# Block 1's one-hot rows: VectorE compares, GpSimd multiplies the columns' side by the weights

## The chip, the cores and the metric

The kernel is one program on one core of a Trainium2 chip. Its time is the device time of one execution in microseconds (us), the median of several executions. The core has five engines with their own instruction streams: TensorE (PE in the profile, its weight loads PEld), VectorE (DVE), ScalarE (ACT), GpSimd (POOL) and SyncE (SP). They work on SBUF, 128 partitions wide, and TensorE writes its results to PSUM. An engine takes its instructions in order, and semaphores tie the engines together. Sixteen DMA engines move data between HBM and SBUF; transfers are issued from the queues of SP and POOL here.

## The reference

One layer of a streaming encoder for 256 tokens of width 2048: a token-mixing part (an SSD branch and an attention branch, gated and merged), then a channel-mixing part. Only the second matters here, and of it only the end:

```python
def peer_ffn(h, w_q, keys_1, keys_2, u_table, v_table):
    ...
    top_score, top_pos = lax.top_k(cand_score, PEER_TOPK)
    expert = jnp.take_along_axis(cand_index, top_pos, axis=-1)   # index = i1 * 128 + i2
    gate = jax.nn.softmax(top_score, axis=-1)
    ...
        u = jnp.take(u_table, e_blk, axis=0)
        act = jax.nn.gelu(jnp.einsum('td,ted->te', h_blk, u), approximate=False)
        v = jnp.take(v_table, e_blk, axis=0)
        return jnp.einsum('te,ted->td', g_blk * act, v)
```

Each token chooses 8 x 16 = 128 of the 128 x 128 experts. Its output is the sum of 128 rows of the table v (16384 rows of 2048 numbers), each times a weight g * act. Everything is float32.

## The kernel before

The 256 tokens are two blocks of 128 (b = 0, 1), a token to a partition. The sum over v is made in two ways, one for each half of the width.

- **The right half (columns 1024 to 2047)** is gathered: for each of the 256 pairs of block and choice, r = 0 to 255, GpSimd issues an indirect DMA (`gather`, L2103, 512 KB) into one of the 8 slots of `vrow`, and VectorE adds the row times its weight to an accumulator in PSUM (`add_row`, L1965 and L1968). Row r can be gathered only once row r - 8 is added (semaphore `vrow_used`).
- **The left half (columns 0 to 1023)** is dense: every row of the table goes through TensorE (L990, 1024 products of 128x512, with units of 1 MB of the table in the 4 slots of `vden`, loaded from SP). The matrix that it is multiplied by, `wt`, holds each token's weight for each of the 16384 experts. It is made here in advance.

`wt` is made token by token. For a token the 128 choices lie on the partitions. Two one-hot matrices are formed, one row to each choice: o[0] has a 1 at column i1 (the rows' side), o[1] at column i2 (the columns' side), and o[1] is then multiplied by the choice's weight. One product of the two, 128x128, is the token's weight matrix. Four tokens (OHT = 4) are a group; a block has 32 groups (OHB = 32), n = 0 to 31. A group's one-hots fill one of two buffers, `oh[b][:, n % 2]`.

For block 0 ScalarE makes the one-hots, and the sum over v waits. For block 1 VectorE does, and its loop is what the change touches. Once block 0 and all rows of the table u are done (the scores' rows `rrow`, L1937), each group of block 1 goes like this:

- VectorE compares (L1981, 128x1024 for both sides of four tokens), waits for its own result (`link`), and multiplies the columns' side by the weights `selT[:, 2]` (L1983, 128x512). That sets `oh_ready`. From n = 2 on the comparison first waits for `wt_done` of group n - 2, since it writes into that group's buffer.
- TensorE takes four products (L981) and sets `wt_done`.
- ScalarE copies the result from PSUM into `wt1a` and `wt1b` (L1331) and sets `wt_read`.
- After every fourth group VectorE adds one gathered row (`add_row(n // 4)`, L1985). GpSimd has issued rows 0 to 7 before, and issues one more behind each added row.

After the last group VectorE runs through the rest of the 256 rows and TensorE through the dense half; the fourth slot of `vden` lies on the one-hots' buffers, so SP loads it only when all products of the one-hots are done. At the end VectorE forms the residual and the last LayerNorm (L1992 to L2014), and SP stores.

Of the kernel before, what the change touches and what calls it, by code (L numbers as in the profile page):

```python
# [12 lines left out]
ALU = mybir.AluOpType  # L13
# [4 lines left out]
P = 128  # L18
D = 2048
SEQ = 256  # L20
BLK = SEQ // P
# [82 lines left out]
class Steps:  # L104
# [14 lines left out]
    def link(self, ins):  # L119
        self.step(ins)  # L120
        self.wait()
# [9 lines left out]
def build(nc, a, out, stop="all"):  # L131
    ctx = ExitStack()
    with ctx:
        KB = 1024

        def at(name, offset, shape, dt=F32):
            return nc.alloc_sbuf_tensor_at(name, shape, dt, offset=SBUF_START + int(offset))
# [10 lines left out]
        def sem(name):  # L148
            return ctx.enter_context(nc.semaphore(name))
# [114 lines left out]
        ROWS = 8  # L264
# [24 lines left out]
        SEL = PEER_HEADS * TOPK  # L289
# [3 lines left out]
        niota = cos2[:, :, :].rearrange("p b n -> p (b n)")  # L293

        selT = at("selT", 206 * KB, [P, 3, P])

        OHT, OHB = 4, P // 4
        oh = [at("oh0", 102 * KB, [P, 2, 2, OHT, P]), at("oh1", 70 * KB, [P, 2, 2, OHT, P])]
# [9 lines left out]
        def wt_column(b, q):  # L308
            return wt[b][0][:, q, :] if b == 0 or q < QA else wt[b][1][:, q - QA, :]
# [37 lines left out]
        ada_in_ready = sem("ada_in_ready")  # L347
        rows_turned = sem("rows_turned")
        cols_ready = sem("cols_ready")
        c_hi_ready = sem("c_hi_ready")  # L350
        c_ready = sem("c_ready")
        x_normed = sem("x_normed")
        x_turned = sem("x_turned")
# [81 lines left out]
        square_done = sem("square_done")  # L435
        hot_done = sem("hot_done")
        oh_ready = sem("oh_ready")
        wt_done = sem("wt_done")
        wt_read = sem("wt_read")

# [21 lines left out]
        dve_step = sem("dve_step")  # L462
        act_step = sem("act_step")
        pool_step = sem("pool_step")
        probe_done = sem("probe_done")

# [9 lines left out]
        def on(phase):  # L478
            return order.index(phase) <= upto
# [120 lines left out]
        def _(pe):  # L600
# [143 lines left out]
            if on("att"):  # L744
                pe.wait_ge(cn_split, 2)
                pe.wait_ge(kpe_read, 1)
                with pe.Fori(0, 4) as i:
                    for k in range(2):
# [10 lines left out]
                        n = (U_ATT + k) % 2  # L759
                        rope = [w[:, n, :, 0:2 * QH].rearrange("p kc (e m) -> p kc e m", e=2)[:, :, :, NOPE:QH]  # L760
                                for w in (whi, wlo)]
                        for b in range(BLK):
                            o = ps[:, 0, 0, b * 256 + k * P:b * 256 + k * P + P]
# [6 lines left out]
                    for k in range(2):  # L770
# [4 lines left out]
                        n = (U_ATT + 2 + k) % 2  # L775
                        val = [w[:, n, :, :].rearrange("p kc (e m) -> p kc e m", e=2)[:, :, :, NOPE:KVH]
                               for w in (whi, wlo)]
                        for b in range(BLK):
                            o = aux[:, b, k * 256:k * 256 + 256]
# [20 lines left out]
                    for h in range(4):  # L800

                        for b in range(BLK):
                            nk = P * (b + 1)
                            o = aux[:, h, b * P:b * P + nk]
# [161 lines left out]
            if on("all"):  # L966
                pe.wait_ge(score_a, 4)
                pe.wait_ge(score_v, 4)
                for b in range(BLK):
                    pe.wait_ge(w_ready, PEER_HEADS * (b + 1))  # L970
                    for k in range(3):
                        src = w_all[:, b * SEL:(b + 1) * SEL] if k == 2 else sides[:, k, b * SEL:(b + 1) * SEL]
                        last = nc.tensor.transpose(aux[:, 2, k * P:k * P + P], src, ident)  # L973
                    last.then_inc(sel_turned, 1)
                    for n in range(OHB):
                        m = b * OHB + n
                        pe.wait_ge(oh_ready, m + 1)
                        if m >= 2:
                            pe.wait_ge(wt_read, m - 1)
                        for t in range(OHT):  # L980
                            last = mm(aux[:, n % 2, t * P:t * P + P], oh[b][:, n % 2, 0, t, :], oh[b][:, n % 2, 1, t, :],  # L981
                                      start=True, stop=True)
                        last.then_inc(wt_done, 1)
                pe.wait_ge(wt_read, BLK * OHB)
                for u in range(NVU):
                    pe.wait_ge(vden_full[u % 4], vden_before[u % 4] + 16 * (u // 4 + 1))
                    for q in range(2):
                        for b in range(BLK):
                            for n in range(DV // W):
                                last = mm(aux[:, 2 * b + n, :], wt_column(b, 2 * u + q),  # L990
                                          vden[:, u % 4, q, n * W:n * W + W],
                                          start=(u == 0 and q == 0), stop=(u == NVU - 1 and q == 1))
                    last.then_inc(vden_used, 1)
# [389 lines left out]
        def _(dve):  # L1383
            V = nc.vector
            S = Steps(dve, dve_step)
            link = S.link
# [277 lines left out]
            if on("mla"):  # L1664
# [6 lines left out]
                with dve.Fori(0, 2) as i:  # L1671
                    S.enter(i, 4 + 2 * (DC - 1))
                    for s in range(2):
# [5 lines left out]
                        for k in range(2):  # L1679
                            m = premix[:, ds(i * 8 + (4 * s + 2 * k), 2), :]  # L1680
# [98 lines left out]
            if on("so"):  # L1779

                dve.wait_ge(g0_ready, 4)
                with dve.Fori(0, 2) as i:
                    S.enter(i, 4)
                    for s in range(2):
# [3 lines left out]
                        for k in range(2):  # L1788
                            m = ds(i * 8 + (4 * s + 2 * k), 2)
# [138 lines left out]
            if on("all"):  # L1928
# [30 lines left out]
                def add_row(r):  # L1959

                    o = ps[:, r // SEL, :, :].rearrange("p a n -> p (a n)")
                    row, w = vrow[:, r % ROWS, :], w_all[:, r:r + 1]
                    dve.wait_ge(vrow_full[r % ROWS], vrow_before[r % ROWS] + 16 * (r // ROWS + 1))
                    if r % SEL == 0:
                        last = V.tensor_scalar(o, row, w, None, ALU.mult)  # L1965
                    else:
                        dve.wait_ge(vrow_used, r)
                        last = V.scalar_tensor_tensor(o, row, w, o, ALU.mult, ALU.add)  # L1968
                    last.then_inc(vrow_used, 1)
# [6 lines left out]
                for n in range(OHB):  # L1976
                    if n >= 2:
                        dve.wait_ge(wt_done, OHB + n - 1)
                    o = oh[1][:, n % 2]
                    t4 = slice(n * OHT, n * OHT + OHT)  # L1980
                    link(V.tensor_tensor(o, niota.unsqueeze(1).unsqueeze(1).broadcast_to([P, 2, OHT, P]),  # L1981
                                         selT[:, 0:2, t4].unsqueeze(3).broadcast_to([P, 2, OHT, P]), ALU.is_equal))
                    V.tensor_tensor(o[:, 1], o[:, 1], selT[:, 2, t4].unsqueeze(2).broadcast_to([P, OHT, P]), ALU.mult)\  # L1983
                        .then_inc(oh_ready, 1)
                    if n % 4 == 3:  # L1985
                        add_row(n // 4)
                for r in range(OHB // 4, BLK * SEL):
# [31 lines left out]
        def _(pool):  # L2019
            G = nc.gpsimd  # L2020
# [79 lines left out]
            if on("all"):  # L2100
                def gather(dst, table, r):
                    pool.sem_inc(held, 1)
                    return G.indirect_dma_start(  # L2103
                        out=dst, out_offset=None, in_=table,
                        in_offset=bass.IndirectOffsetOnAxis(ap=eid_all[:, r:r + 1], axis=0))

                for r in range(BLK * SEL):
                    if r % TOPK == 0:
                        pool.wait_ge(expert_ready, r // TOPK + 1)
                    if r in (0, 1):  # L2110

                        pool.wait_ge(lo_ready, U_END + 3 + r)
                    if r == 4:

                        pool.wait_ge(pe_used, U_END + 2)
                    pool.wait_ge(row_used, r + 1)
                    gather(rrow[:, r % ROWS, :], a["peer_u"][0], r).then_inc(row_full[r % ROWS], 16)
                for r in range(BLK * SEL):
                    if r < ROWS:

                        pool.wait_ge(row_used, ROWS + BLK * SEL - ROWS + r // 2 + 1)
                    else:
                        pool.wait_ge(vrow_used, r - ROWS + 1)
                    gather(vrow[:, r % ROWS, :], a["p_vg"], r).then_inc(vrow_full[r % ROWS], 16)

    return nc

# [45 lines left out]
```

## Time and profile before

| What | Value |
|---|---|
| Median of 3 executions | 2972.63 us (2970.52 to 2976.9) |
| The profiled execution's own time | 2973.76 us |
| Its span, first to last instruction | 2972.0 us |
| Mean granted clock of TensorE | 0.835 of full speed |
| Busy time of PE, DVE, ACT, POOL | 2027.2, 2231.5, 868.8, 911.0 us |

All times in the rows are counted from the span's start. The profiled execution's time is 1.76 us longer than its span. Its granted clock is a share of full speed: 1.0 is the level 2.4 GHz, 0.5 is 1.2 GHz.

### The profile page before, as it was taken

To read this page: it belongs to the slowest core of one execution; us is meant where nothing else is said; L and a number is where in the kernel's file an instruction comes from. 1 tells how busy PE (TensorE), PEld (TensorE's weight loads), DVE (VectorE), ACT (ScalarE), POOL (GpSimd) and SP (SyncE) were. 2 spreads that over 40 slices of the span, in tenths; PEclk is the share of its full clock that TensorE was granted. 3 is DMA by queue.
4 is the path that set the end of the run, shared out by engine and by line. 5 is a ranking of instruction groups with operands and counts; after the bars stand their busy time and mean duration, and the time that the engine had idled before them with its cause. 6 is when DMAs were issued, how large, how long until landed. Compare 5 with 4: busy or idle time off the path is not lost.

```text
span 2972.0 us, 33711 instructions
## 1 busy us (share of the span) xinstructions
PE 2027.2 (68%) x11910; PEld 1659.2 (56%) x11910; DVE 2231.5 (75%) x2576; ACT 868.8 (29%) x1225; POOL 911.0 (31%) x725
## 2 busy tenths in 40 slices
PE   4589998999999999998968000001111269999991
PEld 3589998888888889998768000001111154444440
DVE  7757677788878784445565999999999997666568
ACT  1144442344444444333342000004554620000000
POOL 0000001222222220001001656565656724444343
PEclk9799999999999999999989555555555569999995
DMA  8656668666555554655534888898989949999996
GB/s 340 281 181 203 209 212 307 218 219 208 207 200 205 200 194 170 228 182 213 183 139 188 322 356 342 336 364 330 367 326 366 378 159 367 413 414 414 415 413 235
DMA packets 144932, 817.42 MB, mean 275 GB/s; under 512 B 16520, under 2 KB 21248, under 8 KB 70832
## 3 DMA queue, kind: packets, MB, share of 16 engines
q0 software_dynamic: 93200, 477.21, 41.3%
q1 hardware_dynamic: 49728, 336.05, 30.5%
q10 hardware_dynamic: 1888, 2.59, 0.2%
q8 instruction: 76, 1.25, 0.2%
q14 instruction: 40, 0.33, 0.0%
HBM read 811.55 MB, written 4.23 MB: 274 GB/s over the span
## 4 chain that ended last, share of the span: by engine, by line
PE 38%; DVE 34%; DMA 14%; issue 8%; ACT 2%; POOL 1%; DVEq 1%; ACTq 0%; POOLq 0%
DVE rrow L1937 16%; DMA vrow<-in_p_vg,acc 12%; PE ps L639 9%; PE ps L641 9%; PE ps L640 9%; DVE ps L1968 3%; DVE wlo L1392 2%; DVE acc L1441 2%; ACT whi L1006 2%; PE ps L619 2%; PE ps L621 2%; PE ps L620 2%; DMA ada_in<-in_p_ada 1%; DVE oh L1981 1%; PE aux L898 1%
## 5 line engine op out<-in xcount | busy, mean ns | idle before, releaser
L1392 DVE TENSOR_TENSOR wlo<-raw,whi 128x2048 fp32r<-128x2048 f32 x216 | 507.5, 2352 | 375.6 <-ACT whi L1006 365.5
L2103 POOL DMA_INDIRECT rrow<-in_peer_u,acc x256 | 471.6, 1842 | 490.5 <-DVE dots L1937 205.8
L1006 ACT ACTIVATE whi<-raw 128x2048 fp32r<-128x2048 f32 x216 | 412.8, 1913 | 706.4 <-PE ps L641 483.7
L1937 DVE CUSTOM_DVE_ANT_0 rrow<-rrow,h 128x2048 f32<-128x2048 f32 x256 | 567.7, 2286 | 2.6 <-issue 1.7
L639 PE MATMUL ps<-h_hi,whi 128*128 128x256 f32 (+1 forms) x1568 | 454.5, 290 | 8.2 <-issue 4.2
L1968 DVE SCALAR_TENSOR_TENSOR ps<-vrow,acc,ps 128x1024 f32<-128x1024 f32 x254 | 327.2, 1288 | 162.3 <-DMA vrow<-in_p_vg,acc 144.6
L640 PE MATMUL ps<-h_lo,whi 128*128 128x256 f32 (+1 forms) x1568 | 444.7, 284 | 0.0
L641 PE MATMUL ps<-h_hi,wlo 128*128 128x256 f32 (+1 forms) x1568 | 444.7, 284 | 0.0
L2103 POOL DMA_INDIRECT vrow<-in_p_vg,acc x256 | 248.8, 972 | 315.1 <-DVE ps L1968 233.3
L981 PE MATMUL aux<-oh 128*128 128x128 f32 x512 | 116.0, 401 | 304.6 <-ACT oh L1350 281.8
L639 PEld LDWEIGHTS ps<-h_hi,whi 128*128 128x128 f32 (+1 forms) x1568 | 300.4, 192 | 21.2 <-issue 13.3
L640 PEld LDWEIGHTS ps<-h_lo,whi 128*128 128x128 f32 (+1 forms) x1568 | 300.4, 192 | 4.0 <-issue 3.8
L641 PEld LDWEIGHTS ps<-h_hi,wlo 128*128 128x128 f32 (+1 forms) x1568 | 300.2, 191 | 0.0
L2033 POOL DMA_DIRECT2D ada_in<-in_p_ada x128 | 69.3, 542 | 750.8 <-DVEq L1542 601.3
L973 PE MATMUL aux<-con,sides 128*128 128x128 f32 x4 | 1.4, 442 | 413.1 <-DVE acc L1949 413.1
L981 PEld LDWEIGHTS aux<-oh 128*128 128x128 f32 x512 | 100.7, 293 | 320.3 <-ACT oh L1350 291.4
L990 PE MATMUL aux<-vden,wt 128*128 128x512 f32 x512 | 242.5, 596 | 5.4 <-DMA vden<-in_p_vd 4.7
L973 PEld LDWEIGHTS aux<-con,sides 128*128 128x128 f32 x4 | 0.6, 204 | 413.5 <-issue 398.9
L1441 DVE SCALAR_TENSOR_TENSOR acc<-ada_in,csil,acc 128x512 f32<-128x512 f32 x240 | 203.4, 848 | 25.3 <-DMA ada_in<-in_p_ada 11.7
L990 PE MATMUL aux<-vden,wt1a 128*128 128x512 f32 x384 | 180.4, 592 | 0.0
L619 PE MATMUL ps<-whi,h_hi 128*128 128x512 f32 x320 | 133.6, 418 | 55.7 <-DVE wlo L1392 55.7
L990 PEld LDWEIGHTS aux<-vden,wt 128*128 128x128 f32 x512 | 97.6, 191 | 128.5 <-issue 122.1
(329 smaller groups left out, 4002.4 us busy)
## 6 DMA issues: line engine op xcount, KB each, us to landing
raw<-in_p_in SPq DMA_DIRECT2D x104, 1024.0 KB, 5.1
ada_in<-in_p_ada POOLq DMA_DIRECT2D x128, 512.0 KB
vden<-in_p_vd SPq DMA_DIRECT2D x64, 1024.0 KB, 8.6
ada_in<-in_p_ada SPq DMA_DIRECT2D x32, 1024.0 KB, 10.1
raw<-in_p_so SPq DMA_DIRECT2D x32, 1024.0 KB, 4.9
raw<-in_p_mo SPq DMA_DIRECT2D x16, 1024.0 KB, 6.8
raw<-in_p_bc SPq DMA_DIRECT2D x16, 1024.0 KB, 4.9
raw<-in_p_mix SPq DMA_DIRECT2D x16, 1024.0 KB, 4.9
```

The source lines that it names most:

```text
L619: mm(outs[b], x_hi[:, k, t], hi[:, kc, 0:width], start=(k == 0), stop=False)
L639: mm(o, wh, x_hi[:, k, :], start=(k == 0 and first), stop=False, skip_group_check=True)
L640: mm(o, wh, x_lo[:, k, :], start=False, stop=False, skip_group_check=True)
L641: last = mm(o, wl, x_hi[:, k, :], start=False, stop=(k == klast), skip_group_check=True)
L981: last = mm(aux[:, n % 2, t * P:t * P + P], oh[b][:, n % 2, 0, t, :], oh[b][:, n % 2, 1, t, :], start=True, stop=True)
L990: last = mm(aux[:, 2 * b + n, :], wt_column(b, 2 * u + q), vden[:, u % 4, q, n * W:n * W + W], start=(u == 0 and q == 0), stop=(u == NVU - ...
L1006: F(whi[:, n % 2, :, 0:cols_], raw[:, n % 4, :, 0:cols_], ACT.Copy).then_inc(hi_ready, 1)
L1392: V.tensor_tensor(wlo[:, n % 2, :, 0:cols_], raw[:, n % 4, :, 0:cols_], whi[:, n % 2, :, 0:cols_].bitcast(F32), ALU.subtract).then_inc(lo_ ...
L1441: last = V.scalar_tensor_tensor(acc_, tile[:, kc, :], csil[:, k:k + 1], acc_, ALU.mult, ALU.add)
L1937: last = V.tensor_tensor_reduce(row, row, h2[:, b, :], 1.0, 0.0, ALU.mult, ALU.add, dots[:, k, e:e + 1])
L1968: last = V.scalar_tensor_tensor(o, row, w, o, ALU.mult, ALU.add)
L2103: return G.indirect_dma_start(out=dst, out_offset=None, in_=table, in_offset=bass.IndirectOffsetOnAxis(ap=eid_all[:, r:r + 1], axis=0))
```

## The change

The loop on VectorE keeps the comparison alone and signals it by a new semaphore, `oh_equal`. GpSimd takes the multiplication, waits for `oh_equal`, and signals `oh_weighted`, for which TensorE now waits in block 1. GpSimd's gathers of rows 8 to 14 now stand in between, in places written out by hand: behind the multiplications of groups 5, 9, ..., 29. `oh_ready` belongs to block 0 alone, where n + 1 is the count that was m + 1.

```diff
@@ TensorE
                     for n in range(OHB):
                         m = b * OHB + n
-                        pe.wait_ge(oh_ready, m + 1)
+                        pe.wait_ge(oh_weighted if b else oh_ready, n + 1)
@@ VectorE
                     o = oh[1][:, n % 2]
                     t4 = slice(n * OHT, n * OHT + OHT)
-                    link(V.tensor_tensor(o, niota.unsqueeze(1).unsqueeze(1).broadcast_to([P, 2, OHT, P]),
-                                         selT[:, 0:2, t4].unsqueeze(3).broadcast_to([P, 2, OHT, P]), ALU.is_equal))
-                    V.tensor_tensor(o[:, 1], o[:, 1], selT[:, 2, t4].unsqueeze(2).broadcast_to([P, OHT, P]), ALU.mult)\
-                        .then_inc(oh_ready, 1)
+                    V.tensor_tensor(o, niota.unsqueeze(1).unsqueeze(1).broadcast_to([P, 2, OHT, P]),
+                                         selT[:, 0:2, t4].unsqueeze(3).broadcast_to([P, 2, OHT, P]), ALU.is_equal).then_inc(oh_equal, 1)
@@ GpSimd
-                for r in range(BLK * SEL):
+                def half_row(r):
                     if r < ROWS:
 
                         pool.wait_ge(row_used, ROWS + BLK * SEL - ROWS + r // 2 + 1)
                     else:
                         pool.wait_ge(vrow_used, r - ROWS + 1)
                     gather(vrow[:, r % ROWS, :], a["p_vg"], r).then_inc(vrow_full[r % ROWS], 16)
+
+                for r in range(ROWS):
+                    half_row(r)
+                for n in range(OHB):
+
+                    pool.wait_ge(oh_equal, n + 1)
+                    o = oh[1][:, n % 2, 1]
+                    G.tensor_tensor(o, o, selT[:, 2, n * OHT:n * OHT + OHT].unsqueeze(2).broadcast_to([P, OHT, P]),
+                                    ALU.mult).then_inc(oh_weighted, 1)
+                    if n % 4 == 1 and n > 1:
+                        half_row(ROWS + n // 4 - 1)
+                for r in range(ROWS + OHB // 4 - 1, BLK * SEL):
+                    half_row(r)
```

Two unused semaphores (`c_hi_ready`, `probe_done`) go away.

VectorE, from the first group of block 1 on, before (`cos_60` is the tile that holds the numbers 0 to -127, `oh_165` the one-hots):

```order
1370 L1981 TENSOR_TENSOR oh_165<-cos_60,selT 128x1024 [waits selT_ready,row_used,iota_in,w_ready]
1371 L1983 TENSOR_TENSOR oh_165<-oh_165,selT 128x512 [waits dve_step]
1372 L1981 TENSOR_TENSOR oh_165<-cos_60,selT 128x1024
1373 L1983 TENSOR_TENSOR oh_165<-oh_165,selT 128x512 [waits dve_step]
1374 L1981 TENSOR_TENSOR oh_165<-cos_60,selT 128x1024 [waits wt_done]
1375 L1983 TENSOR_TENSOR oh_165<-oh_165,selT 128x512 [waits dve_step]
1376 L1981 TENSOR_TENSOR oh_165<-cos_60,selT 128x1024 [waits wt_done]
1377 L1983 TENSOR_TENSOR oh_165<-oh_165,selT 128x512 [waits dve_step]
1378 L1965 TENSOR_SCALAR ps<-vrow,acc 128x1024 [waits ada2_full0]
```

The same place now:

```order
1370 L1981 TENSOR_TENSOR oh_165<-cos_60,selT 128x1024 [waits selT_ready,row_used,iota_in,w_ready]
1371 L1981 TENSOR_TENSOR oh_165<-cos_60,selT 128x1024
1372 L1981 TENSOR_TENSOR oh_165<-cos_60,selT 128x1024 [waits wt_done] x2
1373 L1965 TENSOR_SCALAR ps<-vrow,acc 128x1024 [waits ada2_full0]
1374 L1981 TENSOR_TENSOR oh_165<-cos_60,selT 128x1024 [waits wt_done] x4
```

The multiplications and the waits for the comparison's result are gone; what VectorE waits for is the product of two groups back, as before.

GpSimd, from the last gathers of the table u on, before and now:

```order
171 L2103 DMA rrow<-in_peer_u,acc 128x2048 [waits row_used] x15
172 L2103 DMA vrow<-in_p_vg,acc 128x1024 [waits row_used] x8
173 L2103 DMA vrow<-in_p_vg,acc 128x1024 [waits vrow_used] x248
```

```order
171 L2101 DMA rrow<-in_peer_u,acc 128x2048 [waits row_used] x15
172 L2101 DMA vrow<-in_p_vg,acc 128x1024 [waits row_used] x8
173 L2130 TENSOR_TENSOR oh_165<-oh_165,selT 128x512 [waits oh_equal] x6
174 L2101 DMA vrow<-in_p_vg,acc 128x1024 [waits vrow_used]
175 L2130 TENSOR_TENSOR oh_165<-oh_165,selT 128x512 [waits oh_equal] x4
176 L2101 DMA vrow<-in_p_vg,acc 128x1024 [waits vrow_used]
...
187 L2130 TENSOR_TENSOR oh_165<-oh_165,selT 128x512 [waits oh_equal] x2
188 L2101 DMA vrow<-in_p_vg,acc 128x1024 [waits vrow_used] x241
```

The 32 multiplications stand between gather 7 and gather 15, with seven gathers among them, and each waits for its comparison.

## Rows read from the trace of the kernel before

**Rows 1.** Busy time and granted clock by stretch, from block 1's one-hots to the end:

```profile
core 0: us, PE busy (x) PEld busy (x) DVE busy (x) ACT busy (x) POOL busy (x), PEclk, DMA share, GB/s
2388.00:2460.00 72.00, 49.62 (x256) 43.72 (x256) 68.99 (x73) 21.09 (x65) 7.90 (x7) 0.76 0.32 110
2460.00:2890.00 430.00, 425.31 (x987) 188.05 (x988) 269.94 (x210) 1.28 (x1) 196.42 (x210) 1.00 1.02 412
```

**Rows 2.** Timeline of the end, TensorE and VectorE (start, length, engine, ..., count):

```profile
2904.50 1.88 PE L990 MATMUL aux<-vden,wt1b 128*128 128x512 f32 x4
...
2895.82 47.23 DVE L1968 SCALAR_TENSOR_TENSOR ps<-vrow,acc,ps 128x1024 f32<-128x1024 f32 x34 [0.35 <-DMA vrow<-in_p_vg,acc]
2943.16 2.35 DVE L1992 SCALAR_TENSOR_TENSOR fin<-gate2b,ps 128x1024 f32<-128x1024 f32 x2
```

**Rows 3.** Groups of instructions between 2380 and 2620 us (busy, mean ns, idle before):

```profile
L1981 DVE TENSOR_TENSOR oh<-cos,selT 128x1024 f32<-128x1024 f32 x32 | 39.0, 1220 | 3.6 <-PE aux L981 1.8 <-ACT selT L1324 1.8
L1983 DVE TENSOR_TENSOR oh<-oh,selT 128x512 f32<-128x512 f32 x32 | 22.1, 692 | 1.1
```

**Rows 4.** Timeline of block 1's first groups, TensorE at the low clock:

```profile
2387.67 1.23 DVE L1981 TENSOR_TENSOR oh<-cos,selT 128x1024 f32<-128x1024 f32 x1 [1.75 <-ACT selT L1324]
...
2388.93 0.69 DVE L1983 TENSOR_TENSOR oh<-oh,selT 128x512 f32<-128x512 f32 x1
2389.53 1.22 DVE L1981 TENSOR_TENSOR oh<-cos,selT 128x1024 f32<-128x1024 f32 x1
...
2389.68 3.94 PE L981 MATMUL aux<-oh 128*128 128x128 f32 x16 [2.80 <-DVE oh L1983]
...
2391.79 1.23 DVE L1981 TENSOR_TENSOR oh<-cos,selT 128x1024 f32<-128x1024 f32 x1 [0.31 <-PE aux L981]
```

**Rows 5.** Timeline: one group's products at the low clock, one at the full:

```profile
2369.52 2.08 PE L981 MATMUL aux<-oh 128*128 128x128 f32 x8 [3.23 <-ACT oh L1350]
...
2404.68 1.16 PE L981 MATMUL aux<-oh 128*128 128x128 f32 x8 [0.70 <-DVE oh L1983]
```

**Rows 6.** Timeline: the stage's first gather and the comparison beside it:

```profile
2396.71 1.21 DVE L1981 TENSOR_TENSOR oh<-cos,selT 128x1024 f32<-128x1024 f32 x1
...
2397.61 1.13 POOL L2103 DMA_INDIRECT vrow<-in_p_vg,acc  x1 [10.23 <-DVE ps L1965]
```

**Rows 7.** Timeline of the last group, all engines and SP's queue:

```profile
2457.99 22.17 DVE L1968 SCALAR_TENSOR_TENSOR ps<-vrow,acc,ps 128x1024 f32<-128x1024 f32 x16
...
2458.12 1.16 PE L981 MATMUL aux<-oh 128*128 128x128 f32 x8 [0.70 <-DVE oh L1983]
...
2459.39 15.00 SPq L583 DMA_DIRECT2D vden<-in_p_vd  x3
...
2460.07 0.94 POOL L2103 DMA_INDIRECT vrow<-in_p_vg,acc  x1 [7.50 <-DVE ps L1968]
```

**Rows 8.** Lines L2061 (GpSimd) and L1441 (VectorE) of the SSD stage: min/median/max ns:

```profile
L2061 POOL TENSOR_TENSOR rad<-con,adt x32: 1029/1052/3107, 537.4 to 1063.2; 128x512 f32<-128x512 f32 x32
...
L1441 DVE SCALAR_TENSOR_TENSOR acc<-ada_in,csil,acc x240: 737/752/1534, 212.4 to 1109.6; 128x512 f32<-128x512 f32 x120
```

**Rows 9.** Timelines of three places of that stage, VectorE and GpSimd asked apart:

```profile
555.74 2.29 DVE L1392 TENSOR_TENSOR wlo<-raw,whi 128x2048 fp32r<-128x2048 f32 x1 [0.59 <-ACT whi L1006]
...
556.42 2.52 POOL L2061 TENSOR_TENSOR rad<-con,adt 128x512 f32<-128x512 f32 x1
...
583.56 2.29 DVE L1392 TENSOR_TENSOR wlo<-raw,whi 128x2048 fp32r<-128x2048 f32 x1 [2.50 <-ACT whi L1006]
585.77 1.53 DVE L1441 SCALAR_TENSOR_TENSOR acc<-ada_in,csil,acc 128x512 f32<-128x512 f32 x1
...
584.60 2.16 POOL L2070 TENSOR_TENSOR xdt<-x_tok,dtv 128x512 f32<-128x512 f32 x1 [19.64 <-ACT x_tok L1219]
...
744.86 4.36 DVE L1392 TENSOR_TENSOR wlo<-raw,whi 128x2048 fp32r<-128x2048 f32 x1 [1.08 <-ACT whi L1006]
...
745.02 2.04 POOL L2061 TENSOR_TENSOR rad<-con,adt 128x512 f32<-128x512 f32 x2
```

More of the change, by code:

```diff
@@ L349, in build @@
         cols_ready = sem("cols_ready")
-        c_hi_ready = sem("c_hi_ready")
         c_ready = sem("c_ready")
@@ L437, in build @@
         oh_ready = sem("oh_ready")
+        oh_equal = sem("oh_equal")
+        oh_weighted = sem("oh_weighted")
         wt_done = sem("wt_done")
@@ L464, in build @@
         pool_step = sem("pool_step")
-        probe_done = sem("probe_done")
         def unit(name, u, kcs=4):
```

## The prediction

> **What bounds the kernel now.** I read the profile from the end backwards. The last stretch of the timeline [rows 2] shows TensorE done with the dense half at 2904.50 + 1.88 = 2906.4 us, while VectorE is still adding gathered rows: 34 of them without a pause, 47.23 us or 1.39 us each, up to 2943.1. The final LayerNorm follows. So the row stream sets the end, and TensorE has 36.7 us to spare. The table of stretches [rows 1] shows the two before that. From 2460 to 2890 the DMA engines are full (share 1.02, 412 GB/s), since the dense table and the gathered rows come together; VectorE adds 210 rows there, 2.05 us each, not 1.39. From 2388 to 2460, block 1's one-hots, DMA is a third busy and VectorE is busy for 69.0 of 72 us. It is VectorE that bounds this stage.
>
> The row stream proper starts where the stage ends. GpSimd issues the next row at 2460.07, 0.80 us behind the row that VectorE adds after its last group (2457.99 + 1.28) [rows 7]. From there on the same bytes must move, at the same rates. If this start moves by x, the end moves by x; if only TensorE's start moves, the end doesn't, up to 36.7 us. What I price is therefore the time from the first comparison (2387.67) [rows 4] to that issue: 72.4 us before.
>
> **What the change takes away.** 32 multiplications of 0.69 us leave VectorE [rows 3]. A group took 1.26 us (comparison and the wait for its result) plus 0.60 (2388.93 to 2389.53) [rows 4], 1.86 in all. 32 groups make 59.5, seven added rows in between at about 1.2 make 8.4; the other 4.5 us are waits for TensorE, like the 0.31 us at 2391.79 [rows 4], and the edges. If GpSimd's work were free and beside VectorE's, VectorE alone would need 32 x 1.14 + 8.4 = 45 us. It won't be the only limit.
>
> **What it adds: a multiplication on GpSimd.** The nearest row is L2061, the same engine, size and type, with one operand spread along the last axis as here: 1.03 to 1.05 us undisturbed [rows 8]. I take 1.03. The Trainium skill ("GPSIMD Engine Reference", section 3.1) puts a two-input elementwise operation at about 2.6 cycles an element, which for 512 elements at its 1.2 GHz would be an estimate of 1.11 us. By that the sum below would be 1.3 us longer, since one multiplication in two lies on its path. The row decides.
>
> **What it adds: the two engines exclude each other.** This is the step on which the forecast turns. At 555.74 VectorE starts an operation with two SBUF inputs (L1392), which ends at 558.03. GpSimd's multiplication starts in the record at 556.42 and takes 2.52 us, not 1.03: it ends 0.9 us after VectorE's end. At 744.86 it is VectorE that loses: 4.36 us instead of 2.29, ending 2.16 us after the second of GpSimd's two operations [rows 9]. Nor does a queue of VectorE's instructions keep GpSimd out: at 585.77 L1441 stands right behind L1392, yet GpSimd's multiplication ends at 586.76, 0.91 after L1392, and L1441 takes 1.53 us instead of 0.75 [rows 8, 9]. Whoever waits comes next. The Trainium skill says the same of operations with two SBUF inputs ("SBUF — State Buffer", section "Who interferes with whom"), and it speaks against this change: what is moved off VectorE still blocks VectorE. The comparison reads two SBUF tiles, and so does the multiplication. The added rows (`vrow` in SBUF, accumulator in PSUM) have one SBUF tile and I take them to run beside it.
>
> **The cycle of a pair of groups.** With two buffers, the comparison of group n waits for the products of n - 2.
> At the full clock: VectorE compares group n (1.22) and, back to back, n + 1 (1.14). GpSimd has asked for n meanwhile, gets its turn after the second and ends 0.90 later. TensorE starts 0.06 us behind it (as 2389.62 to 2389.68 [rows 4]), needs 1.16 us [rows 5], and VectorE goes on 0.02 us later. Beside the products GpSimd does n + 1. Sum: 1.22 + 1.14 + 0.90 + 0.06 + 1.16 + 0.02 = 4.50 us for two groups, 2.25 for one.
> At the low clock the products take 2.08 us [rows 5], and the two groups fall out of step. The chain of one buffer is 1.22 + 0.10 (a signal to GpSimd, taken as short) + 1.03 + 0.06 + 2.08 + 0.02 = 4.51 for two groups, 2.26 for one, when nobody collides; one collision for each pair adds 0.90, and makes it 2.71. I take the middle, 2.49.
> The stage's mean granted clock was 0.76 [rows 1], so about 52% of it at the full level. With that share kept, a group costs 0.52 x 2.25 + 0.48 x 2.49 = 2.37, and 32 of them 75.7 us, up to the last product.
>
> **What hides.** The seven added rows (1.2 us) run while GpSimd multiplies and TensorE works (0.90 + 1.24 us in each cycle); if that cover were gone they would cost 8.4 us. A gather now stands between the multiplications of a pair and the next. It took 1.13 us in this stage, ending 0.81 after the comparison beside it (2396.71 + 1.21) [rows 6]; with some 0.3 of issue that is 1.4 us, beside two comparisons of 2.36. If uncovered, seven would cost 9.8 us. ScalarE's copies out of PSUM keep their place behind the products. GpSimd has issued its first eight gathers before the first comparison is done.
>
> **The end of the stage.** The last multiplication ends 1.24 before the last product, at 74.5. VectorE's last comparison ended 1.9 before that (0.90 and a second multiplication), so the row added behind it is done at 73.8, and its gather could go 0.80 later, at 74.6. GpSimd itself is free, with 0.3 of issue, at 74.8. Against 72.4 that is +2.4 us. The profiled execution would take 2973.76 + 2.4 = 2976.2; the median shown lies 1.1 below it, so 2975.1, rounded to **2975**. SP's load of the fourth slot of `vden`, now at 2459.39 [rows 7], waits for the last product and comes some 3 us later; it is the fourth unit of the dense half, and TensorE has slack.
>
> **Rivals.**
> - *No exclusion for this pair of operations.* If comparison and multiplication run side by side, the chain of one buffer is 1.22 + 0.10 + 1.03 + 0.06 + 1.16 + 0.02 = 3.59, 1.80 a group at the full clock and 2.26 at the low; mixed 2.02, so 64.6 us to the last product, 63.7 to the gather and -8.7: 2964. Against it stand all places in rows 9. Chance 0.10.
> - *The low clock and collisions take over.* TensorE has 1.16 us of work in 2.25 instead of about 2.1, and the stage of block 0, where it works 2.08 and idles 3.23, ran at the low clock [rows 5]. If the stage stays low with most pairs colliding, 2.6 a group, it is 83.2 us to the last product, 81.3 to the gather (the last products take 2.16 with their signal), +8.9: 2981.5. It decides (over +5.9) from 2.5 a group on. For it speaks that the middle I took is only a middle; against it that at the low clock TensorE would be busy for 2.08 of every 2.6 us, more than before. Chance 0.18.
> - *The multiplication is dearer here than L2061*, being in place and without a spread first operand: at 1.29 instead of 1.03, 16 pairs add 4.2 us: +6.6, 2979. Chance 0.08.
> - *The change doesn't act*, because the stage's length doesn't reach the end. Only TensorE's part has slack; the row stream has none. Folded into the forecast, since it would give the same verdict.
>
> **How the numbers follow.** The forecast, -1 to +6 us, has 0.64. A measurement of this kernel can tell about 0.2%, 5.9 us, from no change. So: faster 0.10 from the first rival; slower 0.26 from the next two; the same 0.64. The bounds of the cycle are 2.25 throughout (71.1 us to the gather, -1.3) and 2.71 throughout (84.9, +12.5). The range leaves the first rival's centre out below and the far end of the collisions above: 2967 to 2983.
>
> **What would show it.** Comparisons recorded at 1.2 or, if they wait, about 2.1 us; multiplications at 1.03 or, waiting, about 1.9 to 2.0, ending 0.90 after a comparison; never both active for long. First comparison to gather 15: about 74.8 us. Groups per 4.5 us at the full clock: two. The 34-row tail at 1.39 us unchanged, and TensorE's end well before VectorE's. I am wrong if the comparisons don't lengthen while the multiplications run, if added rows lengthen, or if a gather holds back the multiplication behind it.

## The result, and the profile after

The changed kernel is slower by a quarter of a per cent: 2981.85 us median (2976.85 to 2985.27, 7 runs) against 2972.64 (2970.52 to 2976.92, 7 runs), ratio of the means 1.0026 with a 95% interval of 1.0014 to 1.0037. A second comparison on another occasion gave 2980.09 us (11 runs) against 2974.0 (15 runs), ratio 1.0019, interval 1.0010 to 1.0028. The forecast was 2975 us, range 2967 to 2983. The profiled execution took 2979.52 us, its span is 2977.6 against 2972.0.

The stretches after, the stage of block 1's one-hots and the one behind it, answer to [rows 1]:

```profile
core 0: us, PE busy (x) PEld busy (x) DVE busy (x) ACT busy (x) POOL busy (x), PEclk, DMA share, GB/s
2385.20:2465.60 80.40, 53.71 (x256) 47.49 (x256) 58.03 (x42) 20.42 (x62) 49.06 (x40) 0.69 0.28 97
2465.60:2895.00 429.40, 424.14 (x978) 187.44 (x978) 269.11 (x209) 1.94 (x3) 196.38 (x211) 0.99 1.02 412
```

VectorE gave up 11 us of work in the stage (58.0 against 69.0), and the stage grew all the same. No engine is busy for its length now: VectorE 58 of 80 us, TensorE 54, GpSimd 49. The stretch behind it has not changed.

The groups of instructions after, of the stage, answer to [rows 3]:

```profile
L981 PE MATMUL aux<-oh 128*128 128x128 f32 x256 | 54.1, 384 | 27.4 <-POOL oh L2130 26.9
...
L1981 DVE TENSOR_TENSOR oh<-cos,selT 128x1024 f32<-128x1024 f32 x32 | 47.3, 1480 | 23.9 <-PE aux L981 22.0 <-ACT selT L1324 1.7
L2130 POOL TENSOR_TENSOR oh<-oh,selT 128x512 f32<-128x512 f32 x32 | 35.5, 1114 | 30.9 <-DVE oh L1981 30.8
```

The 32 comparisons, the same instructions as before, are 8.3 us dearer: 47.3 against 39.0. VectorE waits 22 us for TensorE, TensorE 27 for GpSimd, GpSimd 31 for VectorE: a ring of three in which each waits for the next. VectorE's waits for TensorE were 1.8 us before [rows 3].

The same two lines by source, min/median/max ns:

```profile
L1981 DVE TENSOR_TENSOR oh<-cos,selT x32: 1209/1226/2136, 2385.2 to 2460.6; 128x1024 f32<-128x1024 f32 x32
...
L2130 POOL TENSOR_TENSOR oh<-oh,selT x32: 1030/1040/1947, 2386.6 to 2462.9; 128x512 f32<-128x512 f32 x32
```

14 of the 32 comparisons took 1.42 us or more, and only 5 of the 32 multiplications over 1.1.

The timeline of the first pair, with the low clock, and of the stage's end after:

```profile
2385.25 2.36 DVE L1981 TENSOR_TENSOR oh<-cos,selT 128x1024 f32<-128x1024 f32 x2 [1.75 <-ACT selT L1324]
2386.56 2.94 POOL L2130 TENSOR_TENSOR oh<-oh,selT 128x512 f32<-128x512 f32 x2 [2.85 <-DVE oh L1981]
...
2388.56 3.72 PE L981 MATMUL aux<-oh 128*128 128x128 f32 x16 [4.10 <-POOL oh L2130]
...
2390.67 1.23 DVE L1981 TENSOR_TENSOR oh<-cos,selT 128x1024 f32<-128x1024 f32 x1 [3.06 <-PE aux L981]
...
2462.69 5.45 DVE L1968 SCALAR_TENSOR_TENSOR ps<-vrow,acc,ps 128x1024 f32<-128x1024 f32 x4
...
2464.78 0.97 POOL L2101 DMA_INDIRECT vrow<-in_p_vg,acc  x1 [0.89 <-DVE ps L1968]
```

GpSimd's first two multiplications take 2.94 us for two, though one alone takes 1.04: the first waits until VectorE's second comparison is over at 2387.61, and ends 0.9 us later. From the first comparison to gather 15 it is 2464.78 - 2385.25 = 79.5 us, against 72.4 before (+7.1; forecast +2.4).

The end of VectorE's stream after answers to [rows 2]:

```profile
2897.35 51.41 DVE L1968 SCALAR_TENSOR_TENSOR ps<-vrow,acc,ps 128x1024 f32<-128x1024 f32 x37 [0.32 <-DMA vrow<-in_p_vg,acc]
2948.87 2.35 DVE L1990 SCALAR_TENSOR_TENSOR fin<-gate2b,ps 128x1024 f32<-128x1024 f32 x2
```

The tail is 1.39 us a row, as before. TensorE ends at 2915.9, 33 us ahead of it.

The times of all traces, from the first comparison and gather 15 of each timeline (the mean clock is that of the time up to the last product):

| Kernel | Comparison 0 starts | to the last product | to gather 15 | from there to the end | Clock |
|---|---|---|---|---|---|
| before | 2387.7 | 71.6 | 72.4 | 511.9 | 0.76 |
| before, again | 2385.4 | 71.6 | 72.4 | 512.9 | 0.78 |
| changed | 2385.3 | 80.8 | 79.5 | 512.9 | 0.69 |
| changed, again | 2386.9 | 80.1 | 77.4 | 513.1 | 0.69 |
| changed, operand in PSUM | 2384.7 | 61.9 | 61.6 | 512.8 | 0.88 |
| changed, no gathers inside | 2381.4 | 76.4 | 83.2 | 514.7 | 0.72 |
| before, 32 idle multiplications | 2385.2 | 87.4 | 87.3 | 512.7 | 0.50 |
| changed, four buffers | 2383.5 | 73.1 | 72.0 | 515.6 | 0.76 |
| changed, PSUM and four buffers | 2388.2 | 47.9 | 46.8 | 515.9 | 0.92 |
| before, operand in PSUM | 2382.9 | 71.6 | 72.4 | 512.4 | 0.78 |
| changed, more products | 2386.8 | 75.4 | 75.0 | 512.8 | 0.95 |
| before, four buffers | 2382.3 | 69.2 | 70.0 | 514.5 | 0.79 |

The first column moves by up to 7 us between executions, through work ahead of the stage that no kernel here changes. In single executions it can hide a part of a difference, which is why stages are compared and not spans.

### The profile page after: what moved, and what is told of

It is laid out like the page before. It is cut to its first block, busy times and chain, and to the rows that moved or that the text cites. A ratio compares the mean times of both kernels' runs of the same rounds, so it can differ in the third digit from the quotient of the medians.

```text
span 2977.6 us, 33711 instructions
## 1 busy us (share of the span) xinstructions
PE 2033.1 (68%) x11910; PEld 1662.9 (56%) x11910; DVE 2218.6 (75%) x2544; ACT 869.0 (29%) x1225; POOL 951.0 (32%) x757
## 4 chain that ended last, share of the span: by engine, by line
PE 39%; DVE 33%; DMA 14%; issue 8%; POOL 2%; ACT 2%; DVEq 0%; ACTq 0%; POOLq 0%
DVE rrow L1937 16%; DMA vrow<-in_p_vg,acc 11%; PE ps L639 9%; PE ps L641 9%; PE ps L640 9%; DVE ps L1968 3%; DVE wlo L1392 2%; DVE acc L1441 2%; ACT whi L1006 2%; PE ps L619 2%; PE ps L620 2%; PE ps L621 2%; POOL vrow L2101 1%; DVE ada_acc L1461 1%; DMA ada_in<-in_p_ada 1%
## 5 line engine op out<-in xcount | busy, mean ns | idle before, releaser
L1441 DVE SCALAR_TENSOR_TENSOR acc<-ada_in,csil,acc 128x512 f32<-128x512 f32 x240 | 204.0, 850 | 26.9 <-DMA ada_in<-in_p_ada 13.8
```

The lines of the kernel that those rows point to most:

```text
L1441: last = V.scalar_tensor_tensor(acc_, tile[:, kc, :], csil[:, k:k + 1], acc_, ALU.mult, ALU.add)
```

## The experiments

**One operand of the comparison in PSUM.** A PSUM bank is free in this stage. VectorE copies the numbers there once, and the comparison has one SBUF input.

```diff
                 dve.wait_ge(iota_in, 16)
+                link(V.tensor_copy(aux[:, 3, 0:P], niota))
                 dve.wait_ge(selT_ready, 2)
...
-                    V.tensor_tensor(o, niota.unsqueeze(1).unsqueeze(1).broadcast_to([P, 2, OHT, P]),
+                    V.tensor_tensor(o, aux[:, 3, 0:P].unsqueeze(1).unsqueeze(1).broadcast_to([P, 2, OHT, P]),
```

> The changed kernel, but the comparison reads its first operand (the numbers 0 to -127) from a free PSUM bank, so it has one SBUF input and not two. VectorE copies it there once, before the stage, where it waits anyway. Theory (the two engines exclude each other because both operations read two SBUF tiles): comparisons all take about 1.2 us and multiplications 1.03 to 1.05, side by side; the stage from the first comparison to gather 15 falls from 79.5 to about 64 us (2.0 a group), and the kernel is about 15 us faster than the change and 8 faster than before. Rival (the loss lies in the signals between three engines and in the low clock): the stage stays at 77 to 80 us.

Measured: 2961.85 us median against 2973.84, ratio 0.9960 (0.9946 to 0.9974), and a stage of 61.6 us. The lines of comparison and multiplication by source (min/median/max ns):

```profile
L1982 DVE TENSOR_TENSOR oh<-aux,selT x32: 1215/1225/1225, 2384.6 to 2443.0; 128x1024 f32<-128x1024 f32 x32
...
L2131 POOL TENSOR_TENSOR oh<-oh,selT x32: 1038/1039/1041, 2386.0 to 2444.3; 128x512 f32<-128x512 f32 x32
```

and its first pair, each engine's timeline asked apart:

```profile
2384.65 2.36 DVE L1982 TENSOR_TENSOR oh<-aux,selT 128x1024 f32<-128x1024 f32 x2 [1.30 <-ACT selT L1324]
...
2385.96 2.16 POOL L2131 TENSOR_TENSOR oh<-oh,selT 128x512 f32<-128x512 f32 x2 [1.48 <-DVE oh L1982]
```

In the changed kernel the maxima were 2136 and 1947 ns; here nothing is ever stretched, and the first multiplication starts and ends under the second comparison. One operand's place is worth 16 to 18 us of stage (61.6 against 77.4 and 79.5). The granted clock rose with it, from 0.69 to 0.88, but the clock can't be the cause of so much: with more products for TensorE (below) it was 0.95, and the stage still took 75.0 us. The exclusion is what the change ran into, and the theory of mere signals between three engines, which would have left the stage as it was, falls. At the full clock the ends of multiplications two groups apart lie 3.61 us from each other on average (24 such distances at that clock), where the forecast's first rival had worked out 3.59.

**The same operand in the kernel before**, as its control. The edit is the same.

> The kernel before with the comparison's first operand in PSUM, nothing on GpSimd. It tells whether the gain of the changed kernel with that operand comes from the operand itself. Theory (only the exclusion matters): VectorE's 1.22 and 0.69 us stay, the stage stays at 71 to 73 us, the kernel is the same as before. Rival (an operand in PSUM is quicker for VectorE or for the gathers): comparisons under 1.15 us and a stage under 69 us.

Measured: 2973.76 us median against 2972.13, ratio 1.0009 (1.0000 to 1.0018); the comparison 1.218 us; the stage 72.4. Gathers take 0.94 us in place of 1.13. The operand alone brings nothing; it is worth something only because GpSimd multiplies beside it.

**GpSimd multiplies for nobody.** The kernel before, and behind each group's signal GpSimd multiplies constants by the group's weights into a scratch tile.

```diff
+                    if ROWS <= r < 2 * ROWS:
+                        for n in range(n0, n0 + 4):
+                            pool.wait_ge(oh_ready, OHB + n + 1)
...
+                            G.tensor_tensor(acc[:, 1, :].rearrange("p (t q) -> p t q", t=OHT),
+                                            upper.unsqueeze(1).broadcast_to([P, OHT, P]),
+                                            selT[:, 2, n * OHT:n * OHT + OHT].unsqueeze(2).broadcast_to([P, OHT, P]),
+                                            ALU.mult).then_inc(extra, 1)
```

> The kernel before, and GpSimd does 32 additional multiplications of the same size whose results nobody uses, one behind each group's signal, four and then its gather. Nobody but the last LayerNorm waits for them. Theory (exclusion): VectorE's comparison or multiplication beside each takes about 1 us longer, a group 2.7 to 2.9 us instead of 2.2, the stage from 72.4 to some 90 to 100 us. Rival (no exclusion for these operands): VectorE's durations stay at 1.22 and 0.69 and the stage at 72 to 74 us.

Measured: 87.3 us of stage, and 2987.07 us in the one execution. Its timeline and VectorE's two lines by source:

```profile
2403.05 1.21 DVE L1982 TENSOR_TENSOR oh<-cos,selT 128x1024 f32<-128x1024 f32 x1
...
2403.20 1.95 POOL L2129 TENSOR_TENSOR acc<-con,selT 128x512 f32<-128x512 f32 x1 [0.63 <-DVE oh L1984]
2404.29 1.41 DVE L1984 TENSOR_TENSOR oh<-oh,selT 128x512 f32<-128x512 f32 x1
...
2405.62 1.28 DVE L1969 SCALAR_TENSOR_TENSOR ps<-vrow,acc,ps 128x1024 f32<-128x1024 f32 x1
...
2405.78 1.04 POOL L2129 TENSOR_TENSOR acc<-con,selT 128x512 f32<-128x512 f32 x1 [0.63 <-DVE oh L1984]
```

```profile
L1984 DVE TENSOR_TENSOR oh<-oh,selT x32: 691/1410/1411, 2386.5 to 2469.1; 128x512 f32<-128x512 f32 x32
...
L1982 DVE TENSOR_TENSOR oh<-cos,selT x32: 1209/1212/1226, 2385.2 to 2467.8; 128x1024 f32<-128x1024 f32 x32
```

The idle work waits for the comparison (to 2404.26), ends 0.9 behind it, and VectorE's multiplication is blocked meanwhile: 1.41 us in place of 0.69. The mechanism is as expected, the price is 0.72 us a collision where I gave 1 us. And only 24 of VectorE's 32 multiplications were stretched: every fourth of GpSimd's fell beside an added row (one SBUF input, one in PSUM), and there both kept their usual times, 1.04 and 1.28 us. 24 x 0.72 is 17 us; the stage grew by 15, since some 2 us of waits for products went. That is why it came out shorter than expected. TensorE's granted clock was 0.50 throughout, but it cost nothing: VectorE is busy for 86.6 of 88 us and waits for no product. The stage's end depends on none of these multiplications, so exclusion alone costs 15 us here.

**No gathers between the multiplications.** Rows 8 to 14 are gathered behind the last one.

```diff
-                    if n % 4 == 1 and n > 1:
-                        half_row(ROWS + n // 4 - 1)
-                for r in range(ROWS + OHB // 4 - 1, BLK * SEL):
+                for r in range(ROWS, BLK * SEL):
```

> The changed kernel without the seven gathers between the multiplications: rows 8 to 14 are gathered after the last multiplication, so the kernel as a whole ends later by some 5 us or more, and only the stage up to the last product is to be compared. Theory (each gather holds back the multiplication behind it, since it takes 1.8 to 1.9 us here): the stage falls from 80.4 to 75 us or below. Rival (gathers are hidden beside two comparisons, as forecast): it stays within 2 us of 80.4.

Measured: 76.4 us to the last product, against 80.8 and 80.1 with the gathers. The kernel took 2981.18 us: gather 15 comes at 83.2, since seven gathers stand ahead of it. The expected 75 was missed, but the gathers hold up about 4 us, more than the 2 that would have counted as hidden. It is one trace, and the granted clock differed a little too (0.72 against 0.69), so a part of the 4 us may be the clock's. The timeline of the changed kernel shows how, GpSimd and VectorE asked apart:

```profile
2438.44 1.04 POOL L2130 TENSOR_TENSOR oh<-oh,selT 128x512 f32<-128x512 f32 x1 [1.16 <-DVE oh L1981]
2439.62 1.78 POOL L2101 DMA_INDIRECT vrow<-in_p_vg,acc  x1
2441.43 2.42 POOL L2130 TENSOR_TENSOR oh<-oh,selT 128x512 f32<-128x512 f32 x2
...
2438.53 2.03 DVE L1981 TENSOR_TENSOR oh<-cos,selT 128x1024 f32<-128x1024 f32 x1 [0.17 <-PE aux L981]
2440.73 1.22 DVE L1981 TENSOR_TENSOR oh<-cos,selT 128x1024 f32<-128x1024 f32 x1 [0.17 <-PE aux L981]
```

The gather at 2439.62 ends at 2441.40, 0.84 behind the comparison that ended at 2440.56. So an indirect gather is held up by such a comparison as a multiplication is: 1.78 us here, 0.97 with the operand in PSUM. The multiplication behind it could have started at 2440.64, and starts 0.8 later, under the next comparison, whose end it must wait for: it ends at 2442.85, 0.90 behind it. All seven gathers inside the stage, in both traces of the changed kernel, end 0.84 to 0.85 us behind a comparison.

**Four buffers instead of two.**

```diff
-        oh = [at("oh0", 102 * KB, [P, 2, 2, OHT, P]), at("oh1", 70 * KB, [P, 2, 2, OHT, P])]
+        oh = [at("oh0", 102 * KB, [P, 2, 2, OHT, P]), at("oh1", 62 * KB, [P, 4, 2, OHT, P])]
...
-                    if u == 3:
+                    if u == 2:
...
-                    if n >= 2:
-                        dve.wait_ge(wt_done, OHB + n - 1)
-                    o = oh[1][:, n % 2]
+                    if n >= 4:
+                        dve.wait_ge(wt_done, OHB + n - 3)
+                    o = oh[1][:, n % 4]
```

> The changed kernel with four buffers for block 1's one-hots instead of two (the third slot of the dense table is loaded later too). Theory (with two buffers each group waits in a chain for comparison, multiplication and products; with four only the exclusion is left, 1.09 + 0.90 = 1.99 us a group): the stage is 64 to 70 us, the kernel 10 to 15 us faster than the change and up to 8 faster than before. Rival (exclusion and gathers alone set 2.4 a group): the stage stays at 77 to 80 us.

Measured: 2975.79 us median against 2973.84, ratio 1.0007 (0.9997 to 1.0017), stage 72.0. The stage lies between the two expectations. The kernel is some 6 us faster than the changed one where 10 to 15 were expected, and not faster than the kernel before, since it loses 3 us behind the stage. By source:

```profile
L1981 DVE TENSOR_TENSOR oh<-cos,selT x32: 1210/2055/2884, 2383.5 to 2450.4; 128x1024 f32<-128x1024 f32 x32
...
L2130 POOL TENSOR_TENSOR oh<-oh,selT x32: 1032/1948/2017, 2384.8 to 2454.3; 128x512 f32<-128x512 f32 x32
```

Here the exclusion stands alone: VectorE never waits for a product, its stream is full for 72.7 of 73 us, and the typical comparison and multiplication are recorded at 2.06 and 1.95 us, close to half of it blocked by the other engine. That is near the 1.99 us a group expected above. What I had left out of 64 to 70 is the gathers, 1.78 us each in the same queue: a round of four groups took 9.1 us from gather to gather, not 8.

**The kernel before with four buffers**, the control (the same edit, without GpSimd's part):

> The kernel before with four buffers of one-hots. Its waits for products (the 4.5 us that the forecast found beside VectorE's own work) should go: a stage of 68 to 70 us instead of 72.4. If the third slot of the dense table, loaded later, costs something behind the stage, the time from gather 15 to the end is longer than 512 us here too, as in the changed kernel with four buffers (515.6).

Measured: 70.0 us, 2968.62 us in one execution. Some 2.4 us of VectorE's waits for products went, about half of the 4.5 us that the forecast called waits and edges. The rest is no wait: the stage as measured also holds the eighth added row (1.28 us) and the 0.80 us from it to gather 15.

**More products for TensorE.** After each group of block 1 two products of constants into the free bank.

```diff
                         last.then_inc(wt_done, 1)
+                        if b:
+                            for t in range(2):
+                                mm(aux[:, 3, t * P:t * P + P], ident, upper, start=True, stop=True)
```

> The changed kernel, and behind each group of block 1 TensorE does two more products of constants into a free PSUM bank that nobody reads, only to be busier. Theory (the low clock is a part of the loss, since the groups at it take about 2.6 us against 2.25): the stage's mean granted clock rises from 0.69 towards 0.9 or more and the stage falls from 79.5 by 2 to 5 us, though the additional products can delay a group by up to 0.6 us. Rival (the clock doesn't matter, exclusion and gathers set the pace): the clock rises and the stage stays within 1 us of 79.5 or grows.

Measured: 2974.19 us median against 2972.13, ratio 1.0009 (0.9999 to 1.0018), so the changed kernel's loss can't be told from none. The stage is 75.0 us at a mean granted clock of 0.95 against 0.69, with half as many products more. Its stretch:

```profile
2387.00:2462.00 75.00, 50.16 (x380) 45.97 (x381) 54.73 (x41) 20.42 (x62) 48.08 (x40) 0.95 0.31 110
```

Multiplications two groups apart end 4.58 us from each other on average at the full clock (28 distances), where the forecast had worked out 4.50. But no distance is 4.50: 3.59, 4.80, 5.57 and 4.37 come by turns, a rhythm of four groups with one stretched comparison and one stretched multiplication. In the changed kernel the seven distances that lay wholly at the low clock were 5.08 on average, from 4.51 to 5.71. But the clock is not the only thing that moved: with the engines in this rhythm the gathers fall between comparisons (0.97 us each, not 1.78 to 1.90). The run doesn't part the two.

**Operand in PSUM and four buffers together.**

> Both of the earlier edits: the comparison reads one operand from PSUM, and there are four buffers of one-hots. With the exclusion gone and the chain through the products loosened, the stage should be set by one engine: VectorE 45 us, GpSimd 32 x 1.04 + 7 x 1.2 = 42, TensorE 37 at the full clock and 67 at the low one. Expected 48 to 55 us against 61.6 with two buffers, and a kernel 8 to 12 us faster than that one, less what the later load of the dense table's third slot costs (some 3 us, as the four-buffer kernel showed behind the stage). Rival (TensorE's clock falls, the stage is bound there): 60 us or more.

Measured: 2953.13 us median against 2972.13, ratio 0.9938 (0.9923 to 0.9954), the fastest of all. The stage is 46.8 us. Its stretch and the comparisons by source:

```profile
2388.00:2436.00 48.00, 37.04 (x256) 33.20 (x256) 47.59 (x42) 20.54 (x63) 40.82 (x41) 0.92 0.42 147
```

```profile
L1982 DVE TENSOR_TENSOR oh<-aux,selT x32: 1210/1214/1224, 2388.2 to 2431.6; 128x1024 f32<-128x1024 f32 x32
its engine sat idle before it (us, times) until:
  ACT selT L1324: 1.3, 1
```

VectorE is busy for 47.6 of 48 us and waits for nobody: this is the 45 us that it would need if GpSimd's work were beside its own. It pays 3 us behind the stage (515.9 against 512.8 with two buffers), as all three kernels with four buffers do (2 to 4 us). The later load of the dense table's third slot is the likely reason: an estimate for one more unit of 1 MB behind the stage, at the 412 GB/s that the DMA engines moved there [rows 1], is 2.5 us. It was not tried by itself.

**Both kernels once more.**

> The changed kernel once more, for a second trace and more times. Its median lay 9.2 us above before, its stage in the one trace 7.1 us. Theory (the stage is the only loss, and its length varies with TensorE's clock): the stage is again 77 to 84 us and the time from gather 15 to the end 512 to 513 us, the difference of the medians 5 to 9 us. Rival (something outside the stage loses too): the time from gather 15 to the end, or that up to the stage, is over 2 us longer than in the traces of before.

> The kernel before once more, for a second trace. The stage should again be 72 to 73 us from the first comparison to gather 15, and 512 us from there to the end; the stage's start is what varies, by 3 us or so, as between the traces so far (2381.4 to 2388.2).

Measured: stages of 77.4 (changed) and 72.4 us (before), 513.1 and 512.9 us behind them. Nothing outside the stage lost. The changed kernel's stage itself varies, by 2 us between two traces, while that of before doesn't. The difference of the medians was 9.2 and 6.1 us on the two occasions, that of the stages 7.1 and 5.0; whether the 2 us or so on top of them are chance was not settled.

## Why the prediction was right, and where it was off

The range held the time and the sign of the shift was right, but the loss was 0.26%, where a change within 0.2% had been called likeliest; in the second comparison it was 0.19%. The time of this stage was forecast at +2.4 us and came at +7.1 and +5.0; in the first comparison the median lies just over 1 us inside the upper bound. That it lies inside is partly luck: the range reached so far up for the sake of collisions at the low clock, and most of what the stage's sum lacked came with the gathers. What bounds the kernel and the exclusion were right; a term of the sum was too small, and the cycle's order was another than the one worked out.

- **What sets the end.** Right. From gather 15 to the end it was 511.9 to 513.1 us in the eight traces with two buffers and gathers inside the stage, while the stage ran from 61.6 to 87.3. And only gather 15 counts, not TensorE's start: without gathers inside, the last product came 4 us earlier and gather 15 4 us later, and the kernel was no faster.
- **The multiplication on GpSimd.** 1.04 us alone, forecast 1.03 from [rows 8]. The estimate of 1.11 us from the Trainium skill's 2.6 cycles an element ("GPSIMD Engine Reference", section 3.1) was the worse guess. The rival of a dearer multiplication falls.
- **The exclusion.** Right, and shown by the operand in PSUM. In the changed kernel comparisons took up to 2.1 us, multiplications up to 1.95, ending 0.9 us behind VectorE's end; added rows beside multiplications kept their 1.28. Without it the stage is 61.6 us; the first rival's working gave 63.7 at a granted clock of 0.76, and it was 0.88.
- **The cycle of a pair.** Right on average, not in its order. At the full clock it was 4.58 us a pair (more products), 4.50 forecast. But the forecast let two comparisons run back to back and every second multiplication wait, for 1.9 to 2.0 us. In the first trace of the changed kernel only the first multiplication took that long, and four others 1.35 to 1.43; it was VectorE that lost, with 14 of 32 comparisons at 1.42 to 2.14 us. That the average still fits is in part luck. The chain without a collision was worked out well: 4.51 us at the low clock and 3.59 at the full one both stand in the traces.
- **The step that failed: "What hides".** I took a gather as 1.4 us beside two comparisons of 2.36 us. It takes 1.78 to 1.90 us in this stage, because it too waits for the comparison that it meets, and then holds back the multiplication behind it, which the forecast had named as a sign of being wrong. The row was there: 1.13 us instead of 0.94, ending 0.81 after the comparison beside it [rows 6], which I read as a duration and not as the end of a wait. Without the gathers the last product comes at 76.4 us, where the forecast's cycle, 32 x 2.37, had put it at 75.7. So the gathers explain some 4 of the 4.7 us that were missing in the first trace, together with what they cost in clock.
- **The clock.** I kept the stage's granted clock at 0.76; it fell to 0.69 in both traces, with TensorE idle longer between groups. Low-clock pairs cost 5.08 us (seven), forecast 4.98 (the middle). This and the gathers can't be added up, since either changes the rhythm in which the other strikes. The rival of the low clock and collisions gave 2981.5 us and was to decide from 2.5 us a group on; 2.52 and 2.50 a group were measured, and a median of 2981.85. So its number came, but not as it was worked out: the clock was at the full level for 38% of the time, and without the gathers a group took 2.39.
- **Added rows beside GpSimd.** Right: 1.28 us each under multiplications.

## What to carry to other kernels

Before moving work from VectorE to GpSimd, look at VectorE's operands: where its instruction reads two SBUF tiles, the work moved can still take its time from VectorE. Here a collision cost VectorE 0.72 us, and the multiplication that was moved had cost it 0.69. Putting one operand of VectorE's instruction in PSUM removed that here, for one copy, and turned a loss of 0.26% into a gain of 0.4%. A second buffer pair was worth little in the original kernel (2.4 us of stage) and 15 us of stage once the exclusion was gone; and GpSimd's indirect gathers in the same queue meet the same exclusion.

## What was not expected of the hardware

An indirect gather issued by GpSimd meets the same exclusion against a comparison with two SBUF inputs: 1.78 to 1.90 us, ending 0.8 us behind the comparison's end, against 0.97 with one operand in PSUM (0.94 against 1.13 in the kernel before). With more work on TensorE a stage in which TensorE is waited for came out shorter (75.0 us in one trace, against 79.5 and 77.4), with the granted clock at 0.95 instead of 0.69; how much of it is the clock's and how much the gathers', which fell between comparisons there, is open.
